# Two stages of a two-layer block kernel run head by head in turns instead of one after the other

## The reference

```python
# stick-breaking attention: 8 heads of width 64, 640 positions (128 of lead and meta tokens, then 512)
z = einsum('bhtd,bhsd->bhts', q_block, k[:, :, :t1]) * scale
log_beta = log_sigmoid(z)
log_keep = where(valid, log_sigmoid(-z), 0.0)
log_tail = cumsum(log_keep, axis=3, reverse=True) - log_keep
w = where(valid, exp(log_beta + log_tail), 0.0)
out = einsum('bhts,bhsd->bhtd', w, v)

# gated recurrence: 4 heads of width 128, chunks of 128 positions
bc = cumsum(g, axis=2)                                   # running log decay in a chunk
decay = exp(where(causal, bc[t] - bc[s], -inf))          # per channel
scores = einsum('bhtd,bhsd,bhtsd->bhts', qc, kc, decay)
o = scores @ vc + (qc * exp(bc)) @ state
state = exp(b_last) * state + (kc * exp(b_last - bc)).T @ vc

o_sb = rmsnorm_per_head(out) ; o_hg = rmsnorm_per_head(o) * silu(hg_g)
h = h + concat(o_sb, o_hg) @ w_out                       # then the second mixture of experts
```

## Time and profile before

| what | value |
|---|---|
| median of three runs | 1916.47 us |
| the profiled execution's own time | 1919.64 us |
| its span | 1917.7 us |
| stick-breaking stage, about 1107 to 1232 us of the span | 125 us |
| recurrence stage, about 1232 to 1324 us | 92 us |
| TensorE busy / VectorE busy in the first of the two | 110.1 / 87.6 us |
| TensorE busy / VectorE busy in the second | 60.0 / 68.5 us |
| mean granted TensorE clock in the two | 0.80 and 0.82 of full |

### The profile page before, as it was taken

The page is one execution under the profiler, slowest core; times in us unless marked ns, Lnnn a source line. Parts: engine busy times, 40 slices in busy tenths (PEclk is TensorE's granted clock), DMA queues, the critical chain, the costliest instruction groups (busy, mean ns, idle before and its releaser), DMA issues.

```text
span 1917.7 us, 18800 instructions
## 1 busy us (share of the span) xinstructions
PE 1591.1 (83%) x7524; PEld 1058.5 (55%) x7524; DVE 764.8 (40%) x1212; ACT 334.2 (17%) x555; POOL 263.4 (14%) x286
## 2 busy tenths in 40 slices
PE   5996999897999686977899988877878786888773
PEld 4785888775888332323688857766733232333331
DVE  6899635534364410114622267676420000101003
ACT  3310000115101110101311167432100000000001
POOL 0102003300000310101200014652020000000001
PEclk9998999999999797988899968988979998999997
DMA  4221232120246899998222100101789999999994
GB/s 174 76 99 66 66 103 96 66 88 1 66 153 250 263 401 427 427 427 338 91 83 80 58 1 1 45 1 46 310 276 429 429 431 428 429 431 429 430 418 163
DMA packets 54820, 412.05 MB, mean 215 GB/s; under 512 B 13888, under 2 KB 15168, under 8 KB 25936
## 3 DMA queue, kind: packets, MB, share of 16 engines
q1 hardware_dynamic: 45008, 394.05, 51.4%
q0 software_dynamic: 9728, 16.81, 2.4%
HBM read 402.40 MB, written 25.20 MB: 223 GB/s over the span
## 4 chain that ended last, share of the span: by engine, by line
PE 49%; DMA 26%; DVE 11%; ACT 4%; issue 4%; POOL 3%; SPq 2%; POOLq 0%; DVEq 0%; ACTq 0%
PE bank L1364 31%; PE bank L582 6%; DMA arena<-in_expert_in 5%; DMA ring<-in_expert_gate 5%; DMA ring<-in_expert_up 5%; PE bank L592 3%; DMA arena<-in_expert_gate 2%; DMA arena<-in_expert_up 2%; DMA arena<-in_expert_down 2%; DMA ring<-in_expert_down 2%; DMA arena<-in_expert_out 1%; DVE arena L2060 1%; DVE top L2059 1%; DVE ring_low L1955 1%; PE bank L1479 1%
## 5 line engine op out<-in xcount | busy, mean ns | idle before, releaser
L582 PE MATMUL bank<-arena 128*64 128x512 f32 x960 | 286.5, 653 | 84.9 <-DMA arena<-in_expert_up 22.2
L582 PEld LDWEIGHTS bank<-arena 128*64 128x64 f32 x960 | 97.3, 150 | 256.5 <-issue 254.0
L582 PE MATMUL bank<-ring,arena 128*64 128x512 f32 x576 | 183.9, 624 | 25.0 <-issue 8.7
L830 DVE TENSOR_TENSOR arena<-misc,bank 128x256 f32<-128x256 f32 (+1 forms) x32 | 17.7, 554 | 449.2 <-PE bank L582 306.7
L1954 DVE CAST ring_high<-ring 128x2048 fp32r<-128x2048 f32 x60 | 75.9, 1265 | 261.4 <-DMA ring<-in_stream_a 158.2
L1955 DVE TENSOR_TENSOR ring_low<-ring,ring_high 128x2048 fp32r<-128x2048 f32 x60 | 140.8, 2347 | 2.1
L592 PE MATMUL bank<-arena 128*64 128x512 f32 x448 | 114.4, 595 | 20.2 <-issue 12.8
L1364 PE MATMUL bank<-ring_low,xn_high 128*128 128x512 f32 x288 | 113.1, 393 | 0.0
L1364 PE MATMUL bank<-ring_high,xn_low 128*128 128x512 f32 x288 | 112.6, 391 | 0.0
L1364 PE MATMUL bank<-ring_high,xn_high 128*128 128x512 f32 x288 | 112.5, 391 | 0.0
L582 PEld LDWEIGHTS bank<-ring,arena 128*64 128x64 f32 x576 | 60.8, 144 | 88.9 <-issue 88.9
(11 more groups left out here) (372 smaller groups left out, 2954.2 us busy)
## 6 DMA issues: line engine op xcount, KB each, us to landing
ring<-in_stream_a SPq DMA_DIRECT2D x42, 1024.0 KB, 5.0
arena<-in_expert_gate SPq DMA_DIRECT2D x20, 2048.0 KB, 28.1
arena<-in_expert_up SPq DMA_DIRECT2D x20, 2048.0 KB, 28.7
arena<-in_expert_in SPq DMA_DIRECT2D x19, 2048.0 KB, 30.1
arena<-in_expert_down SPq DMA_DIRECT2D x18, 2048.0 KB, 28.8
ring<-in_expert_up SPq DMA_DIRECT2D x12, 2048.0 KB, 31.3
ring<-in_expert_down SPq DMA_DIRECT2D x12, 2048.0 KB, 28.2
ring<-in_expert_gate SPq DMA_DIRECT2D x12, 2048.0 KB, 30.3
```

What stands on the lines that cost most here:

```text
L582: last = nc.tensor.matmul(h[side * SLOTS:(side + 1) * SLOTS, :], tokens[:, k, side * SLOTS:(side + 1) * SLOTS], w[:, k * 512:(k + 1) * 512 ...
```

## The change

The 28 steps of the recurrence no longer follow the 8 stick-breaking heads; both are put in one loop of nine turns, on every engine. A turn i has four places. Turns 1 to 7 hold four recurrence steps each, one at the end of each place: step 4(i-1)+place. The stick-breaking work of a turn is spread over the places, and the pipeline between heads is shorter: in turn i come the scores of head i and, in the same turn, the sums, the exp and the product with v of head i-1.

| place | TensorE | VectorE | ScalarE | GpSimd |
|---|---|---|---|---|
| 0 | scores(i), step | read scores(i), abs(i), step | exp(i), step | square(i-2), step |
| 1 | sums behind(i-1), step | decay scan(i) for i=1..3, step | ln(i), step | step |
| 2 | step | subtract(i-1), head sums(i-2), softplus(i), step | exp of weights(i-1), high part(i), step | step |
| 3 | times v(i-1), step | step | copy out(i-1), step | low part(i), norm(i-2), step |

Turn 8 has the rest: the last recurrence head's output, and the sums and the product of head 7. The banks are split: five (0 to 4) for the stick-breaking units, three (5 to 7) for the recurrence's. `zw` goes from four buffers to two, the high and low parts from two to one, and the recurrence's working tiles move to other places in SBUF, so that they don't share memory with the heads. The log decay scans and the keys are made in turns 0 to 3. The last head that is normed on VectorE is now stick-breaking head 7.

```diff
     def bank(self, key):
-        return self.index[key] % BANKS
+        return self.place[self.index[key]]
...
+STICK_BANKS, STATE_BANKS = (0, 1, 2, 3, 4), (5, 6, 7)
+PLACES = 4
+STEPS = HGH * LEVELS
+assert STEPS == PLACES * (SBH - 1)
+def step_after(i, place):
+    return PLACES * (i - 1) + place if 1 <= i < SBH else None
...
-        zw = [at(arena, i * STICK, [STICK]) for i in range(3)] + [at(misc, 1024, [STICK])]
-        sps = [x_flat[:, i * STICK:(i + 1) * STICK] for i in range(2)]
-        sp_high = part("sp_high", ring_place[0], 0, [2, STICK])
-        sp_low = part("sp_low", ring_place[1], 0, [2, STICK])
+        zw = [at(arena, i * STICK, [STICK]) for i in range(2)]
+        sps = [at(arena, 2 * STICK, [STICK]), at(misc, 1024, [STICK])]
+        sp_high = part("sp_high", ring_place[0], 0, [1, STICK])
+        sp_low = part("sp_low", ring_place[1], 0, [1, STICK])
...
                 if n == first + 2 * len(STREAM2) - 3:
-                    sp.wait_ge(psum_filled2, U2.filled(("SO", SBH - 1)))
+                    sp.wait_ge(psum_filled2, U2.filled(("R", SBH - 1, NT2 - 1)))
```

TensorE's loop:

```diff
+            for i in range(SBH + 1):
+                for place in range(PLACES):
+                    if place == 0 and i < SBH:
+                        scores(i)
+                    if place == 1 and i >= 1:
+                        sums_behind(i - 1)
+                    if place == 3 and i >= 1:
+                        stick_out(i - 1)
+                    if step_after(i, place) is not None:
+                        step(step_after(i, place))
+                    if i == SBH and place == 0:
+                        head_out(HGH - 1)
+            pe.wait_ge(heads_normed, HGH + 2)
```

A step on ScalarE, then on VectorE:

```diff
+            def step(n):
+                h, lv = divmod(n, LEVELS)
+                if lv == LEVELS - 1 and h + 1 < HGH:
+                    head_exps(h + 1)
+                if n + 1 < STEPS:
+                    level_exp(n + 1)
...
+            def step(n):
+                h, lv = divmod(n, LEVELS)
+                if lv == 0:
+                    if h == 0:
+                        dve.wait_ge(keys_ready, 1)
+                    head_products(h)
                 level_products(n)
                 if n >= 1:
                     level_read(n - 1)
```

GpSimd's step and the end of its loop:

```diff
-            pool.wait_ge(psum_filled2, U2.filled(("SO", SBH - 1)))
-            pool.wait_ge(carried, HGH * NT2)
-            for n in range(HGH * LEVELS):
+            def step(n):
                 h, lv = divmod(n, LEVELS)
+                if n + 2 < STEPS:
+                    level_diff(n + 2)
+                if h >= 1 and lv == 3:
+                    out_square(h - 1)
+                if h >= 1 and lv == 6:
+                    out_norm(h - 1)
...
+                    if place == 3 and i < SBH:
+                        stick_low(i)
+                    if place == 3 and i >= 2:
+                        head_norm(i - 2)
+                    if step_after(i, place) is not None:
+                        step(step_after(i, place))
```

More of the change, by code:

```diff
@@ L96, in __init__, with add @@
     def __init__(self):
-        self.index, self.reader = {}, []
-    def add(self, key, reader):
+        self.index, self.reader, self.place, self.turn = {}, [], [], {}
+    def add(self, key, reader, banks=tuple(range(BANKS))):
         assert key not in self.index, key
+        turn = self.turn.get(banks, 0)
+        self.turn[banks] = turn + 1
         self.index[key] = len(self.reader)
         self.reader.append(reader)
+        self.place.append(banks[turn % len(banks)])
     def bank(self, key):
-        return self.index[key] % BANKS
+        return self.place[self.index[key]]
     def filled(self, key):
@@ L116, in read_before @@
     def read_before(self, key):
-        old = self.index[key] - BANKS
-        if old < 0:
+        i = self.index[key]
+        earlier = [n for n in range(i) if self.place[n] == self.place[i]]
+        if not earlier:
             return None, 0
+        old = earlier[-1]
         who = self.reader[old]
@@ L249, in second_block_units @@
     u.add("hf_meta", "act")
[L250 to L269, removed]
+    for i in range(SBH + 1):
+        for place in range(PLACES):
+            if place == 0 and i < SBH:
+                for s in range(NT2):
+                    u.add(("Z", i, s), "dve", STICK_BANKS)
+            if place == 1 and i >= 1:
+                for s in range(NT2):
+                    u.add(("R", i - 1, s), "dve", STICK_BANKS)
+            if place == 3 and i >= 1:
+                u.add(("SO", i - 1), "act", STICK_BANKS)
+            n = step_after(i, place)
+            if n is not None:
+                step(n)
+            if i == SBH and place == 0:
+                u.add(("HO", HGH - 1), "act_state", STATE_BANKS)
     for k in range(KC):
@@ new lines, in stick_out @@
+            def stick_out(g):
+                pe.wait_ge(weight_ready, g + 1)
+                b = begin2(("SO", g))
+                for t in range(NT):
+                    for s in range(t + 2):
+                        a = STICK_AT[s] + (t - FIRST_T[s]) * P
+                        last_ = nc.tensor.matmul(b[:, t * SBD:(t + 1) * SBD], zw[g % 2][:, a:a + P],
+                                                 sbv[:, s, g * SBD:(g + 1) * SBD], start=(s == 0), stop=(s == t + 1))
+                end2(last_)
@@ new lines, in step @@
+                end2(last_)
+                if lv == 2:
+                    wait_read2(pe, ("KT", h))
+                    b = begin2(("KV", h))
+                    for t in range(NT):
+                        last_ = nc.tensor.matmul(b[:, t * P:(t + 1) * P], kdR[:, h % 2, t * P:(t + 1) * P],
+                                                 hv[:, t, h * HD:(h + 1) * HD], start=True, stop=True)
+                    end2(last_)
+                if lv == 1 and h >= 1:
+                    head_out(h - 1)
```

409 lines of the change are left out of this document (216 added, 193 removed).

## The result

Four runs of the changed kernel gave 1929.71 to 1935.14 us, median 1930.82; four of the kernel before gave a median of 1917.73. The ratio is 1.0075, 95% interval 1.0056 to 1.0093: slower, by 13.1 us. The profiled execution took 1935.14 us (span 1933.2), against 1919.64.

What follows compares the result with a forecast made beforehand. No engine was full; a head's chain of waits set the turn. 1122.6 + 1.0 + 193.2 + 18.0 put the transposes at 1334.8, 10.8 later; 9 taken, 1916.5 + 9 = 1925.5 us, 8 in 10 within 1898 to 1947.

Steps and rivals of the forecast that it cites:

- TensorE before: Kernel before, a head's turn: a loop of 14 us over VectorE and ScalarE, with TensorE not in it.
- The length behind the transposes stays: Behind the transposes of `mixed`: the tail keeps its length, so a microsecond ahead of them is one in the whole.
- Seven turns of 27.6: Joined loop, turns 1 to 7: 24.6 us each at full clock plus 3.0 for the clock, 193.2 in all.
- First half of the turn: Joined turn, from reading scores through level products, level n, sums, subtraction and head sums to softplus: ends at 13.0 us.
- Second half: Joined turn after softplus: high part, low part 4.0 us stopping VectorE's products, level n+3, first score piece, ending at 22.2.
- The clock: TensorE in the joined turn: sums and level n begin at half clock, costing 3.0 us a turn; mean clock near 0.80.
- Tail of the stage: After the seven turns, from HO to the transposes: 16.4 us plus 1.6 for the clock, 18.0.
- The wait of the last weight loads, and the split banks: Last weight loads waiting for the last sums, and banks split between heads and recurrence: both cost nothing.
- The clock holds: Rival on TensorE's clock in the joined loop: without the clock's cost, 13.6 us earlier, 1903 us; chance 0.20.
- the low part doesn't stop the products: Rival on GpSimd's low part beside VectorE's level products: 3 us a turn less, 1904 us; chance 0.10.
- TensorE becomes the bound: Rival in the joined turns: clock stays at 0.50, three of seven turns at 36 us, 1950 us; chance 0.12.
- Nothing to see: Rival on the joined turn: 26.3 us against today's 27 for a head and four steps, 1916.5 us; chance 0.20.

Runs made afterwards that it cites:

- e1: The changed kernel with GpSimd's low part of a head cut into four instructions instead of one: 1927.41 us.
- e9: The changed kernel with two constant matmuls ahead of TensorE's wait for the level products at places 0, 2 and 3: 1915.6 us.
- e4: The changed kernel with the next head's scores issued right behind the product with v, ahead of level n+3: 1911.19 us.
- e2: The changed kernel with its new buffers, split banks and shorter pipeline, but the two stages one after the other again: 1952.05 us.
- e10: e2 with the next scores issued ahead of the product with v, which gets a bank apart from the scores: 1925.23 us.
- e8: The kernel before with the low-part half of the sums behind left out: 1915.66 us.
- e12: The changed kernel with next scores ahead of level n+3, constant matmuls ahead of levels at places 0 and 2, low part in four: 1896.19 us.

## Why the prediction came out right, and where its working did not

The forecast was 1925.5 us, 9 more than the median then known; measured were 13.1 more (1930.82). Against the profiled execution it said 1928.6, and 1935.14 came. The direction, the place and roughly the size of the turn held; the path through the turn's second half did not, and that the size came out near all the same is in part luck: two terms were too large and a third was missing.

- **TensorE before: misread.** The working said that TensorE isn't in the loop of a head's turn. That holds for the part that it read (1158 to 1172), but not for the whole stage: at 1151.58 and from 1177 on, the chain holds products, scores and sums (the rows above and the earlier trace rows), 43 of 117 us.
- **The length behind the transposes stays: nearly.** Transposes 17.3 us later went with 15.5 us in the profiled time.
- **Seven turns of 27.6: nearly.** Level n+3 of turn 7 ended at 1320.5, where the working had 1316.8 for the end of its turns. Turn 1 took 32.1 and the turns 2 to 6 averaged 28.3. I had given turn 1 one microsecond extra; it took about 3 more. It begins with the absolute value that took 4.23 us in place of 1.09 (shown above). Then come the head's keys, diagonal and first level (1128.4 to 1134.1) ahead of its sums. Yet in e1, where that absolute value took 1.39, turn 1 is only 0.9 shorter (31.3): there the chain runs through the low part itself, 6.15 us in four pieces, and the level differences that stand behind it in GpSimd's list.
- **First half of the turn: right.** The absolute value, the level products, level n on TensorE, the sums right behind it (1134.14 behind a level that ended there; 1245.26 behind level and chunk state), subtraction, head sums, softplus. All in the order given. The sums took 4.7 to 6.6 us from the first start to the last end, not always over 6.
- **Second half: the wrong path.** I had high part, low part, stop on VectorE, level n+3. The stop came in six of seven turns, 3.7 to 4.2 us each, so the mechanism was right, but in turns 4 to 7 a product with v of 3.1 to 5.9 us covered it. e1 prices the stop in this kernel at 3.6 us in the whole, not some 3 a turn. Where it was covered, the chain was level n+2, product, level n+3, scores: all TensorE. The working had no product in it and only 0.8 us of scores.
- **The clock: mis-sized.** I expected 0.80 and 3.0 us a turn; it was 0.73. I had let the clock act on the sums and level n only; the product (5.9 against 3.1) and the scores (5.9 against 3.2) were at half as well. e9 gives 15.4 us for lifting the clock to 0.91, with the stop still there; the working had 22.6 (seven times 3.0, and 1.6 at the end) for 0.80. So the clock acted on more pieces than I had counted, and still no run gives it more than its term; the stop cost far less than its own. What filled the gap is TensorE's list, in which product and next scores stand behind the levels: moving the scores alone gave 18.2 us (e4). Such prices, each taken with the rest left as it is, don't add up to the whole.
- **Tail of the stage: 18.0 forecast, 20.8 measured** (1320.5 to 1341.3). The last product with v took 6.00 and not 3.1.
- **The wait of the last weight loads, and the split banks: no cost to be seen.** The scores wait for nothing (0.0 us idle in their group above), the product with v only for its weights (2.2), so no bank holds them up; and behind the transposes nothing was lost.
- **Rivals.** "The clock holds" and "the low part doesn't stop the products" both fell. "TensorE becomes the bound" was half of the truth: its mechanism (TensorE as the chain, at a low clock: 0.62 in turn 5, 0.71 to 0.83 in turns 1 to 4 and 0.80 in turn 6) decided turns such as the fifth, at 30.8 us and not at 36. "Nothing to see" fell with the interval. The 1885 us for the first two together comes to 1882 by its own terms.

What I didn't see at all is that most of the price lay in an edit that I had handled only as part of the turn: the shorter distance between heads. e2 shows it alone at 35.8 us, from which the joining takes 22.7 off, and e10 shows that 28.7 of them go when the next scores are issued ahead of the product. The whole path from scores to product, which before was spread over four turns, now must end within the turn that follows. What stays open: whether the joined loop with the old, longer pipeline would win outright (not tried), what the sums and the clock were worth in the stick-breaking part of the kernel before, and why single turns differ (27.2 to 30.8 us), beyond that the longest, turn 5, has the lowest clock.

## What to carry to other kernels

When stages are merged to fill idle engines, count separately what the merge needs: here the buffers were paid with a pipeline two turns shorter, which cost more than the merge gave. In an in-order queue, put work whose inputs are ready (the next scores) ahead of work that waits (a level, a product), even if it is needed later; that alone was worth 18 to 29 us here. And when an engine takes more of the path, price every piece of it at the clock that its new rhythm gets; a few constant matmuls into a bank that is about to be overwritten can buy that clock back, and smaller stalls may show their price only then. When work is taken away to price it, look whether the engine's busy time fell: in e8's profile the clock had taken the saving back.

## What the runs showed of the hardware

- Added work made TensorE's path shorter: six constant matmuls a turn took the stage's clock from 0.72 to 0.91 and 15.4 us off the kernel. In the kernel before, 28 of them moved the recurrence's clock from 0.82 to 0.94 and the time not at all.
- Less work made TensorE's clock lower: with 120 of its matmuls gone, the stick-breaking part of the kernel before ran at 0.62 in place of 0.80, and TensorE was busy as long as with them (e8's profile, one execution).
- In turn 5 TensorE was busy 16.03 of 16.40 us (1254 to 1270.4), on levels, the product with v and the scores, and its granted clock was 0.50 in all of them; it had been idle for the 2.48 us before. In e12 the corresponding stretch (1235.4 to 1243.5) ran at 1.00; there the engine had been busy in all of the 10.5 us from 1220.9 to 1231.4, and in 3.24 of the next 4.0.
- One GpSimd instruction of 3.97 us held a VectorE instruction of 0.42 for 4.19. Cut in four (1.25 us each on average) the longest hold on the same line was 1.35. The absolute value of 1.09 us was held to 4.23 as well, and to 1.40 beside the cut one (e12).
